# Recurrence of a hybrid decoder trunk: when its outputs are normalised, and where the out-projection's sums stand

## The reference

```
att[t,s] = sum_d q[t,d] k[s,d] exp(b[t,d] - b[s,d])      for s <= t within a chunk
o[t]     = sum_s att[t,s] v[s]  +  (q[t] exp(b[t])) @ state
state    = exp(b_last) * state  +  sum_s (k[s] exp(b_last - b[s])) v[s]
y[t]     = o[t] / sqrt(mean(o[t]^2) + eps) * gain * silu(g[t])
x       += concat(attention, y) @ w_out
```

## Time and profile before

| | us |
|---|---|
| median of 3 runs | 2714.78 (2711.61 to 2716.91) |
| the profiled execution | 2711.42 |
| its span | 2709.7 |
| PE busy | 2499.4 (92%) |
| DVE busy | 1616.1 (60%) |
| ScalarE busy | 1051.9 (39%) |
| POOL busy | 1280.0 (47%) |

### The profile page before, as it was taken

The page is one execution under the profiler, slowest core; times in us unless marked ns, Lnnn a source line. Parts: engine busy times, 40 slices in busy tenths (PEclk is TensorE's granted clock), DMA queues, the critical chain, the costliest instruction groups (busy, mean ns, idle before and its releaser), DMA issues.

```text
span 2709.7 us, 31273 instructions
## 1 busy us (share of the span) xinstructions
PE 2499.4 (92%) x11133; PEld 1985.0 (73%) x11133; DVE 1616.1 (60%) x2354; ACT 1051.9 (39%) x1741; POOL 1280.0 (47%) x674
## 2 busy tenths in 40 slices
PE   6899798799778899999999989989988999999999
PEld 4677676355777688888888877766677888888887
DVE  6478568984886454445554755666444446544483
ACT  4255687556443433222232145435443222322220
POOL 4201233676763265556665712125515466655591
PEclk7999898799899899999999999988999999999999
DMA  4211123000300211112210222202002122111211
GB/s 148 51 28 28 32 67 91 15 8 13 117 16 1 63 55 39 34 58 62 62 46 24 70 98 55 63 16 74 24 19 60 47 62 62 54 37 33 62 62 62
DMA packets 164002, 136.57 MB, mean 50 GB/s; under 512 B 22969, under 2 KB 137730, under 8 KB 163906
## 3 DMA queue, kind: packets, MB, share of 16 engines
q1 hardware_dynamic: 152658, 124.58, 15.3%
q10 hardware_dynamic: 11248, 10.75, 1.5%
HBM read 116.17 MB, written 13.63 MB: 48 GB/s over the span
## 4 chain that ended last, share of the span: by engine, by line
PE 73%; DVE 10%; issue 8%; ACT 4%; POOL 2%; DMA 0%; ACTq 0%; DVEq 0%; POOLq 0%
PE ps L2150 22%; PE ps L2151 21%; PE ps L2152 21%; ACT signs L1218 1%; PE ps L2345 1%; PE ps L2504 1%; POOL cl L892 1%; PE ps L2262 1%; PE ps L2353 1%; DVE ub L2043 1%; DVE QL L1785 1%; PE ps L2333 1%; DVE ps L1723 1%; POOL w_lo L723 1%; DVE ps L1804 1%
## 5 line engine op out<-in xcount | busy, mean ns | idle before, releaser
L2150 PE MATMUL ps<-h_hi,w_hi 128*128 128x512 f32 x1680 | 670.8, 399 | 13.6 <-POOL w_lo L741 9.7
L2151 PE MATMUL ps<-h_lo,w_hi 128*128 128x512 f32 x1680 | 659.8, 393 | 0.0
L2152 PE MATMUL ps<-h_hi,w_lo 128*128 128x512 f32 x1680 | 659.4, 392 | 0.0
L2150 PEld LDWEIGHTS ps<-h_hi,w_hi 128*128 128x128 f32 x1680 | 319.4, 190 | 83.2 <-issue 14.4
L723 POOL TENSOR_TENSOR w_lo<-w_raw,w_hi 128x1024 fp32r<-128x1024 f32 x73 | 193.4, 2650 | 381.9 <-ACT w_hi L1228 376.9
L2151 PEld LDWEIGHTS ps<-h_lo,w_hi 128*128 128x128 f32 x1680 | 319.6, 190 | 67.8 <-issue 3.9
L2152 PEld LDWEIGHTS ps<-h_hi,w_lo 128*128 128x128 f32 x1680 | 318.9, 190 | 68.0
L2040 DVE TENSOR_TENSOR x_res<-ps,x_res 128x1024 f32<-128x1024 f32 x224 | 268.9, 1221 | 115.4 <-PE ps L2152 115.4
L2021 DVE TENSOR_TENSOR u_all<-ps,u_all 128x512 f32<-128x512 f32 x112 | 77.4, 691 | 416.0 <-ACT u_all L1125 416.0
L741 POOL TENSOR_TENSOR w_lo<-w_raw,w_hi 128x1024 fp32r<-128x1024 f32 x112 | 267.1, 2402 | 104.4 <-ACT w_hi L1114 104.4
L2150 PE MATMUL ps<-w_hi,uo_hi 128*128 128x512 f32 x784 | 307.5, 392 | 3.0 <-DVE shared L2040 3.0
(11 more groups left out here) (349 smaller groups left out, 4519.9 us busy)
## 6 DMA issues: line engine op xcount, KB each, us to landing
w_raw<-in_mlp_w_up SPq DMA_DIRECT2D x64, 512.0 KB, 4.0
w_raw<-in_mlp_w_down SPq DMA_DIRECT2D x64, 512.0 KB, 3.8
w_raw<-in_even_w_in SPq DMA_DIRECT2D x23, 512.0 KB, 3.7
x_res<-in_x SPq DMA_DIRECT2D x16, 512.0 KB, 8.8
w_raw<-in_odd_w_in SPq DMA_DIRECT2D x10, 512.0 KB, 3.6
scr_x<-x_res SPq DMA_DIRECT2D x8, 512.0 KB, 2.6
x_res<-scr_x SPq DMA_DIRECT2D x8, 512.0 KB, 4.3
out<-x_res SPq DMA_DIRECT2D x8, 512.0 KB, 2.6
```

What stands on the lines that cost most here:

```text
L2150: t_.matmul(out_, ah, bh, start=first, stop=False)
L2151: t_.matmul(out_, ah, bl, start=False, stop=False)
L2152: return t_.matmul(out_, al, bh, start=False, stop=last)
```

## The change

The squares of a chunk's outputs go to SBUF, over the used keys of that chunk (`kf[:, d, :]`), and the outputs themselves are copied, not yet normalised, to `o_sum` by ScalarE, so bank 5 is free. The sums of squares are kept per chunk in `o_ss`. Roots are taken for four chunks at a time, at slots 34 and 62. Chunks 0 to 3 are normalised, turned, gated and split in the slots of chunks 5 to 8; chunks 4 to 7 after the loop, their turning done by PE between the first tiles of the out-projection, in banks 7, 5, 6 and 7. Low halves move from DVE to POOL. The key factor's subtraction becomes the bias of four exponentials of 128 columns on ScalarE. Turned keys move to bank 7. The attention's sums have bank 4 alone; they stand in slots 2 and 5 of chunks 1 to 7 and two slots behind, and DVE adds each at the end of the fourth slot behind it. The loop ends three slots earlier.

```diff
+o_ss, o_sd = rq[:, 0:32], rq[:, 32:64]
...
-L_KL_ARG, L_KL_EXP, L_KL_PROD, L_KL_TURN, L_KL_COPY = 0, 2, 3, 4, 6
+L_KL_EXP, L_KL_PROD, L_KL_TURN, L_KL_COPY = 2, 3, 4, 6
 L_QE_EXP, L_QE_PROD, L_LAST, L_SPLIT = 4, 5, 6, 6
-R_OUT, R_SQUARE, R_STATE, R_ROOT, R_NORM, R_TURN, R_GATE, R_HIGH, R_LOW = 1, 4, 5, 6, 7, 6, 9, 10, 11
+R_OUT, R_SQUARE, R_STATE = 1, 4, 5
 READ_LAG = 3
-HG_SLOTS = 7 * T + R_LOW + 1
+ROOTS = {7 * 4 + 6: 0, 7 * T + 6: 4}
+N_NORM, N_TURN, N_GATE, N_HIGH, N_LOW = 36, 36, 39, 40, 41
+LAST_BANK = {4: 7, 5: 5, 6: 6, 7: 7}
+HG_SLOTS = 7 * T + 9
+def normed_chunk(n, first):
+    d, rem = divmod(n - first, 7)
+    return d if rem == 0 and 0 <= d < 4 else None
...
-OA_SLOTS = [7 * c + l for c in range(2, T) for l in (0, 2)] + [7 * T + l for l in (0, 2, 4, 5)]
-OA_LAG = 3
+OA_SLOTS = [7 * c + l for c in range(1, T) for l in (2, 5)] + [7 * T + l for l in (1, 4)]
+OA_LAG = 4
...
+    def normed_low(d):
+        dk = slice(d * P, (d + 1) * P)
+        pool.wait_ge(hg["o_hi"], d + 1)
+        g.tensor_tensor(h_lo[:, 4:8, dk], chunk_values(o_den, d), h_hi[:, 4:8, dk].bitcast(F32), ALU.subtract) \
+            .then_inc(hg["o_lo"], 1)
     for n in range(7 * T):
...
             split_low(U_OUT0 + 4 + c // 2 - 1)
+        d = normed_chunk(n, N_LOW)
+        if d is not None:
+            normed_low(d)
     split_low(U_OUT0 + 7)
+    for d in range(3, T):
+        normed_low(d)
     pool.wait_ge(hg["att_read"], 8 * T)
...
         act.wait_ge(hg["att"], 8 * c + 1)
+        act.wait_ge(hg["o_ss"], c + 1)
         round_weights(U_OUT0 + 4 + i)
+    def normed_high(d):
+        act.wait_ge(hg["o_full"], d + 1)
+        s.activation(h_hi[:, 4:8, d * P:(d + 1) * P], chunk_values(o_den, d), ACT.Copy).then_inc(hg["o_hi"], 1)
...
-                act.wait_ge(hg["kl_arg"], c + 1)
-                s.activation(ek[:], ek[:], ACT.Exp, scale=-1.0).then_inc(hg["kl_exp"], 1)
+                if c:
+                    act.wait_ge(hg["kl_turned"], c)
+                for h in range(4):
+                    ins = s.activation(ek[:, h * P:(h + 1) * P], bT[:, h, tk], ACT.Exp, scale=-1.0,
+                                       bias=bT[:, h, c * P + P - 1:c * P + P])
+                ins.then_inc(hg["kl_exp"], 1)
             if l == L_QE_EXP:
...
                     act.wait_ge(hg["s_done"], c)
-                s.activation(klT[:], ps[:, 4, :], ACT.Copy).then_inc(hg["klT"], 1)
+                s.activation(klT[:], ps[:, 7, :], ACT.Copy).then_inc(hg["klT"], 1)
         d = after_chunk(n, R_SQUARE)
...
-            act.wait_ge(hg["o"], d + 1)
-            if d:
-                act.wait_ge(hg["o_full"], d)
-            s.activation(ps[:, 7, :], ps[:, 5, :], ACT.Square).then_inc(hg["o_sq"], 1)
-        d = after_chunk(n, R_ROOT)
+            act.wait_ge(hg["s_done"], d + 1)
+            s.activation(kf[:, d, :], ps[:, 5, :], ACT.Square).then_inc(hg["o_sq"], 1)
+            s.activation(chunk_values(o_sum, d), heads(ps[:, 5, :]), ACT.Copy).then_inc(hg["o_out"], 1)
+        if n in ROOTS:
+            d = ROOTS[n]
+            act.wait_ge(hg["o_ss"], d + 4)
+            s.activation(o_sd[:, 4 * d:4 * d + 16], o_ss[:, 4 * d:4 * d + 16], ACT.Sqrt, scale=1.0 / P, bias=epsc[:]) \
+                .then_inc(hg["o_sd"], 1)
+        d = normed_chunk(n, N_HIGH)
         if d is not None:
...
+            normed_high(d)
         if l == L_SPLIT and c >= 2 and c % 2 == 0:
             round_last(c // 2 - 1 if c < T else 3)
+    for d in range(4, T):
+        normed_high(d)
...
-    def add_and_norm(phase, g0):
+    def add_and_norm(phase, g0, after_first=None):
...
                     add_bank(g0 + 2 * t + hf, t, hf, first_bank(phase))
+                if t == 0 and after_first is not None:
+                    after_first()
                 norm_tile(phase, t)
...
+    def invert_roots(d):
+        r = o_sd[:, 4 * d:4 * d + 16]
+        dve.wait_ge(hg["o_sd"], d // 4 + 1)
+        own.link(v.reciprocal(r, r))
+    def normed(d):
+        o = chunk_values(o_sum, d)
+        dve.wait_ge(hg["o_out"], d + 1)
+        v.tensor_tensor(o, o, o_sd[:, 4 * d:4 * d + 4].unsqueeze(2).to_broadcast((P, 4, P)), ALU.mult) \
+            .then_inc(hg["o_norm"], 1)
+    def gated(d):
+        dve.wait_ge(hg["o_turned"], d + 1)
+        dve.wait_ge(*chunk_landed(d))
+        v.scalar_tensor_tensor(out=chunk_values(o_den, d), in0=heads(ps[:, LAST_BANK.get(d, 7), :]),
+                               scalar=cT[:, R_GB:R_GB + 1], in1=chunk_values(o_den, d),
+                               op0=ALU.mult, op1=ALU.mult).then_inc(hg["o_full"], 1)
     for n in range(HG_SLOTS):
...
                 .then_inc(att["o_norm"], 1)
-        if n - OA_LAG in OA_SLOTS:
...
         if c < T:
...
                             ALU.subtract).then_inc(hg["diff"], 1)
-            if l == L_KL_ARG:
-                if c:
-                    dve.wait_ge(hg["kl_turned"], c)
-                last = bT[:, :, c * P + P - 1:c * P + P].to_broadcast((P, 4, P))
-                v.tensor_tensor(heads(ek[:]), bT[:, :, tk], last, ALU.subtract).then_inc(hg["kl_arg"], 1)
         d = after_chunk(n, R_STATE)
...
             ins.then_inc(hg["s_ready"], 1)
-            dve.wait_ge(hg["s_ready"], d + 1)
-            if d:
-                dve.wait_ge(hg["o_sd"], d)
             dve.wait_ge(hg["o_sq"], d + 1)
-            v.tensor_reduce(ss[:, 0:4], heads(ps[:, 7, :]), AX_X, ALU.add).then_inc(hg["o_ss"], 1)
-        d = after_chunk(n, R_NORM)
+            v.tensor_reduce(o_ss[:, 4 * d:4 * d + 4], heads(kf[:, d, :]), AX_X, ALU.add).then_inc(hg["o_ss"], 1)
+        d = normed_chunk(n, N_NORM)
         if d is not None:
...
+            if d == 0:
+                invert_roots(0)
+            normed(d)
+        d = normed_chunk(n, N_GATE)
         if d is not None:
...
+            gated(d)
...
                               heads(ps[:, i % 4, :])).then_inc(hg["att_read"], 1)
-    add_and_norm(1, G_OUT0 + 16)
+        if n - OA_LAG in OA_SLOTS:
+            i = OA_SLOTS.index(n - OA_LAG)
+            dve.wait_ge(x_landed[i // 2], 32)
+            dve.wait_ge(down_done, G_OUT0 + i + 1)
+            part = x[:, i // 2, i % 2 * HT:(i % 2 + 1) * HT]
+            v.tensor_tensor(part, ps[:, 4, :], part, ALU.add).then_inc(x_added, 1)
+    invert_roots(4)
+    for d in range(4, T):
+        normed(d)
+    for d in range(4, 7):
+        gated(d)
+    add_and_norm(1, G_OUT0 + 16, lambda: gated(7))
...
                      bank0=first_bank(phase))
+            if t == 0:
+                for d in (4, 5, 6):
+                    turn_normed(d)
+            if t == 1:
+                turn_normed(7)
             if t == 2:
...
+    TURNS = [N_TURN + 7 * d for d in range(4)]
+    def turn_normed(d):
+        bank = LAST_BANK.get(d, 7)
+        pe.wait_ge(hg["klT"], min(TURNS[d] // 7 + (TURNS[d] % 7 >= L_KL_TURN), T) if d < 4 else T)
+        pe.wait_ge(hg["o_norm"], d + 1)
+        if bank == 7:
+            pe.wait_ge(hg["o_full"], 5 if d == 7 else d)
+        elif bank == 5:
+            pe.wait_ge(hg["o_out"], T)
+        else:
+            pe.wait_ge(hg["s_ready"], T)
+        for h in range(4):
+            ins = t_.transpose(ps[:, bank, h * P:(h + 1) * P], chunk_values(o_sum, d)[:, h, :], ident[:])
+        ins.then_inc(hg["o_turned"], 1)
     for n in range(HG_SLOTS):
...
                 pe.wait_ge(hg["kl"], c + 1)
-                if c:
-                    pe.wait_ge(hg["klT"], c)
-                added = sum(m < n for m in OA_SLOTS)
-                if added:
-                    pe.wait_ge(x_added, G_OUT0 + added)
+                turned = sum(m < n for m in TURNS)
+                if turned:
+                    pe.wait_ge(hg["o_full"], turned)
...
-                    ins = t_.transpose(ps[:, 4, hs], ek[:, hs], ident[:])
+                    ins = t_.transpose(ps[:, 7, hs], ek[:, hs], ident[:])
                 ins.then_inc(hg["kl_turned"], 1)
...
                 pe.wait_ge(hg["s_ready"], d)
-                pe.wait_ge(hg["o_norm"], d)
+                pe.wait_ge(hg["o_out"], d)
             else:
...
             ins.then_inc(hg["s_done"], 1)
-        d = after_chunk(n, R_TURN)
+        d = normed_chunk(n, N_TURN)
         if d is not None:
-            pe.wait_ge(hg["o_norm"], d + 1)
...
+            turn_normed(d)
         if n in OA_SLOTS:
...
             pe.wait_ge(x_added, G_OUT0 + i)
-            pe.wait_ge(hg["klT"], min(c, T))
             for k in range(4):
...
```

More of the change, by code:

```diff
@@ L353, in build @@
         hg = {n: sem("hg_" + n) for n in (
[L354 to L355 removed]
+            "diff", "exp", "prod", "att", "att_read", "kl_exp", "kl", "kl_turned", "klT", "qe_exp", "qe",
+            "last_exp", "o", "o_sq", "o_out", "o_ss", "o_sd", "o_norm", "o_turned", "o_full", "o_hi", "o_lo", "s_done",
             "s_ready")}
@@ L1365, in _ @@
                             act.wait_ge(hg["s_done"], c)
-                        s.activation(klT[:], ps[:, 4, :], ACT.Copy).then_inc(hg["klT"], 1)
```

(65 more changed lines are left out.)

2 lines of the change are left out of this document (removed).

## The result

The changed kernel takes 2679.39 us, median of four runs (2674.38 to 2680.03), beside 2715.85 for the kernel before on the same chip: a ratio of 0.9865, 95% interval 0.9847 to 0.9883. The forecast was 2679.8, with a range of 2667 to 2698. The profiled execution of after has a span of 2678.2 us, before 2709.7. Engines by the page (busy us and share): PE 2496.1 (93%), DVE 1607.3, ScalarE 1046.1, POOL 1292.8. PE is busy as long over the whole program (2499.4 before) and waits less. Inside the seven intervals between state sums it is busy 124.3 us before and 116.1 after, and idle 35.5 and 10.7.

The account below looks back on a forecast made before the run. Waits between engines bound the recurrence, PE the out-projection. Seven intervals fall from 159.8 to 126.5 us (33.3 saved), the tail saves 1.7: 35 in all, from a median of 2714.78 to 2679.8 us, range 2667 to 2698.

Parts of the forecast that it names:

- What bounds the stage: Chunked recurrence: waits between engines in one loop through four, no engine full; about 7 us of a 23.8 us chunk idle or stretched.
- (1) The loads' price: ScalarE's queue: two table loads fewer per chunk let POOL and PE go on about 2.6 us sooner.
- only the loads go: Rival: the loop re-forms elsewhere, a chunk lasts 21.3 us, 18 us saved, 2697 us; chance 0.24.
- (2) ScalarE's added pieces: ScalarE in a chunk: four short exponentials and an output copy, about 9 us of work, cost nothing unless PE runs ahead.
- (3) DVE: DVE in a chunk: passes removed leave some 15 us in the middle, between 12.1 and 18.5; chunks 5 to 7 add more.
- (4) The addition's place: DVE's addition at the end of the fourth slot behind the out-projection sum: removes 34.2 us of DVE's waiting.
- The new wait: PE's slot-5 sum waits for DVE's addition of slot 2's sum: nothing to 1.7 us, taken as 0.9 a chunk.
- (5) POOL's floor of 16.7: POOL in a chunk: nine products contended with DVE, plus half a weight piece, allow no chunk under 16.7 us.
- PE alone bounds: Rival: chunks shrink to PE's own work, 15.8 to 16.3 us, 49 to 53 us saved, 2664 us; chance 0.08.
- (6) The tail: Out-projection behind the eighth state sum: 26.2 us to the turn for the norm, 1.7 us saved.
- Signals: Expected in the trace: state sums 17 to 19 us apart, four or so table loads, PE over 90% busy, POOL's products nearer 1.6.
- two signs that I had named for being wrong: In the recurrence: intervals over 21 us, or PE idle ahead of the slot-5 sum with DVE as releaser.

## Why the prediction was right, and where it was not

- **What bounds the stage: right.** No engine full, a loop through four; PE waits less by 21.7 for POOL, DVE by 30.6 for PE.
- **(1) The loads' price: wrong as a term of its own.** I had them at 2.6 a chunk, and my rival "only the loads go" at 18 us. Alone they gave 1.2 of stage and no measurable time; put back in the changed kernel they cost 1.3 to 5.1. POOL's 3.72 of waiting in the earlier trace rows was real. Without the loads PE was idle 6.1 us less in seven intervals, and its slower matmuls took 4.9 of that back. They are worth 8 only in between: addition moved, DVE not yet unloaded. I also read the 3.85 us from the first load to the next exponential as the root's; 1.04 of them are ScalarE's rounding of weights (778.37), which stands there in every second chunk only.
- **(2) ScalarE's added pieces cost nothing: as far as shown, right.** It is busy 8.3 to 9.3 us in five of the first six stretches, as written, and 12.5 in the one with the roots; 12.8 us of loads more cost 1.3 to 5.1.
- **(3) DVE: mis-sized.** I put it in the middle at 15 a chunk; the first four stretches of after have 15.5 to 17.6, 16.6 in the mean, and the two with normalising 19.5 and 16.4, where I had 16.3 to 17.4. I counted its relief as cover only, but the key argument alone is 5 to 7 us of the 35: it is a term.
- **(4) The addition's place: right, and undervalued.** Its waits are gone (34.2 to 3.6), and it alone is half of the gain (18.3 of 35.5), where I had given it no price of its own beside the loads'. The new wait is there, 2.6 in three of the seven intervals where I had 0.9 in each, 6.3 together, and 0.85 in the tail as written. But the one of 1.77 in the seventh stands in an interval 4.4 longer than with the sums in slots 1 and 5, where that wait is gone. With POOL's weights in slot 1 the same wait stood and the clock stayed up, and that interval was 3.2 longer and not 4.4. So the lower clock is some 1.2 us of it, and the larger part lies in the wait and what moved with it.
- **(5) POOL's floor of 16.7: wrong.** It has half a weight piece in every chunk, but a piece stands only in the third, fifth and seventh interval; and it takes all products as contended, 1.70 from start to start. The level products took 1.49 in the mean, hardly more than before (1.46), and POOL was busy 14.7 an interval. In the earlier trace rows I took the durations beside DVE for the usual ones. Two intervals ran in 16.5 and 15.8. The second is PE's floor of 15.8 exactly: there the rival "PE alone bounds" was true. In the first PE, DVE and POOL were all full. Full exclusion, by the Trainium skill's page "SBUF — State Buffer" (Who interferes with whom), would by the durations alone be 9 x 1.25 + 2.82 + 7 x 0.6 = 18.3 in the third chunk (an estimate); it took 17.7, and a stretch cut at the state sums is not exact enough to hold that against the rule. In the second, without the weight piece, the same working gives 15.5 (an estimate), and 15.8 was measured with PE full: there it bound nothing. No run here settles the rule.
- **The intervals.** Forecast 18, 18, 18, 19.3, 19.0, 18.7, 15.5; measured 16.5, 15.8, 17.7, 18.5, 21.4, 17.9, 19.0. Sum 126.5 and 126.8. The first four are 4.8 less, the rest 5.1 more: two errors of equal size with opposite signs, so the closeness of the sum is in part luck. I had no term for the clock. It fell in just the two intervals that came out long; in the fifth, 16 matmuls at the lower clock took 1.8 more. Nor did I say that the clock would pay part of the gain: it was 0.91 to 0.93 in every interval before. Of the 33.0 saved in the seven intervals 24.8 are idle time of PE and 8.2 are busy time, though its work grew by some 0.8 (an estimate: one sum of 2.8 more, four turnings of 0.5 fewer). The first interval had one sum before, not none as I wrote (712.53 to 715.35 us in the trace of before); no term of mine rests on that.
- **(6) The tail: right.** 26.2 worked out from the eighth state sum to the turn for the norm, 852.71 - 826.60 = 26.1 measured; PE 47.10 busy of 47.10. To the MLP's weights 2.1 saved, 1.7 forecast.
- **Signals.** Additions without idle ahead (two of sixteen wait), three loads for 13, no gap ahead of the norm's turns: as written. PE over 90% in four of seven. The root group shows (POOL waits 3.69 at 762.14). Three of seven intervals are between 17 and 19, two under that. POOL's products did not near 1.6. And two signs that I had named for being wrong are there in part: one interval over 21 (21.4), and PE idle ahead of the slot-5 sum with DVE as releaser, in three intervals.

Open stays what the later normalising and the own bank bring by themselves: with all else done, 1.9 us at most, which one execution of each kernel does not settle.

## What to carry to other kernels

When two waits of a loop look alike in size, take each away alone and both together: the loads gave 1, the order of DVE's queue 18, and only after it the loads 8. In this kernel it paid to let an in-order engine evacuate a bank behind its feeding work, at the point where its next read has to wait for a later product anyway. As soon as the waits are gone, look which engine has become full and take a pass off that one, and look at the granted clock of each stretch, since slower matmuls behind a wait of PE can cost as much as the wait.

## What the runs showed of the hardware that I had not expected

- A wait of PE can be paid twice. Behind 1.77 us of waiting, eight matmuls started 0.43 apart instead of 0.23; behind 2.46, sixteen took 3.76 instead of 1.95. But with POOL's weights in slot 1, 1.77 and 1.76 at the same kind of place left them 0.23 apart. What decides is not shown.
- A gain elsewhere can be given back in the main so: without table loads the granted clock of a chunk fell from 0.93 to 0.86, PE was idle 6.1 us less in seven intervals and busy 4.9 more, and the time stayed.
- Ten table loads of 1.28 us more, 13 us of ScalarE, moved the stage by 1.3 us, and its first six intervals together by 5.1.
- DVE at 99% of a stretch (21.13 of 21.30) did not lower the clock of PE at 80%: it stayed at 1.00, though PE waited 1.74 and 1.77 in it.
